# A decoder layer with 32 experts on one core: expert products in blocks of 32 slots on four column strips, and two parts of the routing stage moved into the branch stage

## The reference, cut to what matters

```python
merged = sigmoid(gate_a) * y_a + sigmoid(gate_b) * y_b
x = x + g1 * (merged @ w_out)
h2 = rms_norm(x, norm2_w) * (1 + sc2) + sh2
logits = h2 @ w_router + b_router              # 32 experts
top_val, top_idx = top_k(logits, 4); top_w = softmax(top_val)
# for each expert e, on the tokens that chose it
gate = min(h2 @ w_gate[e] + b_gate[e], 7.0)
up = clip(h2 @ w_up[e] + b_up[e], -7.0, 7.0)
y_e = ((up + 1) * gate * sigmoid(1.702 * gate)) @ w_down[e] + b_down[e]
x = x + g2 * sum_e(top_w * y_e); y = rms_norm(x, final_norm_w)
```

## Time and profile before

| what | value |
|---|---|
| median of 3 runs | 2026.03 us (2024.24 to 2029.33) |
| the profiled execution | 2019.1 us, its span 2017.4 us |
| mean granted TensorE clock | 0.929 of full speed |
| PE busy | 1803.5 us (89%) |
| DVE, ACT, POOL busy | 637.8, 301.3, 126.1 us |
| read from HBM | 486.86 MB, 245 GB/s over the span |

### The profile page before, as it was taken

One profiled execution on the slowest core, in us unless ns is written; L12 is line 12 of the kernel. 1 busy time (PEld: TensorE's weight loads), 2 busy tenths in 40 slices (PEclk: granted clock), 3 DMA queues, 4 the chain that ended last, 5 costly groups with the idle time before them and its releaser, 6 DMA issues. The chain is left out here.

```text
span 2017.4 us, 22708 instructions
## 1 busy us (share of the span) xinstructions
PE 1803.5 (89%) x8638; PEld 940.3 (47%) x8639; DVE 637.8 (32%) x1142; ACT 301.3 (15%) x521; POOL 126.1 (6%) x198
## 2 busy tenths in 40 slices
PE   6997998999879994589999999999999999999996
PEld 4775766868446762553333333333333333333332
DVE  1454333361410024733133333322332212232222
ACT  2234131110111001121011111111110100111002
POOL 1111202112100005200000000000000000000000
PEclk8998999997689997699998999999999999999997
DMA  9352162210255332049899999998999779898720
GB/s 325 129 167 84 42 233 101 84 53 1 61 184 206 117 147 96 0 192 421 311 379 414 421 422 422 422 422 342 417 417 390 298 292 365 311 410 336 250 83 28
DMA packets 114943, 494.07 MB, mean 245 GB/s; under 512 B 9931, under 2 KB 27532, under 8 KB 65687
## 3 DMA queue, kind: packets, MB, share of 16 engines
q1 hardware_dynamic: 112906, 490.69, 62.8%
q10 hardware_dynamic: 1984, 2.64, 0.4%
HBM read 486.86 MB, written 6.43 MB: 245 GB/s over the span
## 5 line engine op out<-in xcount | busy, mean ns | idle before, releaser
L1710 PE MATMUL ps_moe<-ring,hT_moe 128*64 128x512 f32 x1280 | 308.6, 641 | 0.0
L1710 PE MATMUL ps_moe<-ext,xg 128*64 128x512 f32 x1280 | 281.8, 595 | 3.5 <-DVE xg L1809 3.5
L1710 PE MATMUL ps_moe<-ring,xg 128*64 128x512 f32 x1280 | 281.7, 595 | 0.0
L739 PE MATMUL ps_mix<-hT,ring 128*128 128x320 f32 x896 | 263.2, 450 | 14.7 <-ACT cbuf L656 6.7
L739 PEld LDWEIGHTS ps_mix<-hT,ring 128*128 128x128 f32 x896 | 174.9, 198 | 90.7 <-issue 15.8
L1710 PEld LDWEIGHTS ps_moe<-ring,hT_moe 128*64 128x64 f32 x1280 | 95.4, 147 | 187.6 <-issue 185.0
L1710 PEld LDWEIGHTS ps_moe<-ext,xg 128*64 128x64 f32 x1280 | 91.8, 137 | 180.5 <-issue 177.5
L1710 PEld LDWEIGHTS ps_moe<-ring,xg 128*64 128x64 f32 x1280 | 89.2, 137 | 178.4 <-issue 178.3
L1836 DVE TENSOR_SCALAR gate<-ps_moe 128x1024 f32<-128x1024 f32 x32 | 39.2, 1224 | 233.7 <-PE ps_moe L1717 233.7
L1845 DVE TENSOR_SCALAR hid<-ps_moe 128x512 f32<-128x512 f32 x64 | 44.0, 687 | 209.8 <-PE ps_moe L1717 209.8
L1822 DVE TENSOR_SCALAR chosen<-ones,expert_row 96x64 bf16<-96x64 f32 x32 | 8.0, 250 | 313.8 <-PE ps_moe L1717 313.8
(11 more groups left out here) (354 smaller groups left out, 1711.1 us busy)
## 6 DMA issues: line engine op xcount, KB each, us to landing
ext<-in_w_gate SPq DMA_DIRECT2D x128, 1024.0 KB, 9.9
ring<-in_w_up SPq DMA_DIRECT2D x128, 1024.0 KB, 10.9
ring<-in_w_down SPq DMA_DIRECT2D x128, 1024.0 KB, 8.4
ring<-in_w_in SPq DMA_DIRECT2D x18, 2048.0 KB, 9.1
ring<-in_w_ada SPq DMA_DIRECT2D x12, 2048.0 KB, 9.3
ext<-in_state_gdn_rec SPq DMA_DIRECT2D x8, 512.0 KB, 8.4
out_rec_sample<-ext SPq DMA_DIRECT2D x8, 512.0 KB, 3.2
ring<-in_w_branch_b SPq DMA_DIRECT2D x2, 2048.0 KB, 15.0
```

The costliest lines, as they stand in the source:

```text
L739: last = nc.tensor.matmul(out, ring[:, place(i), k, P * j:P * j + P], rhs[:, k, :], start=k == 0, stop=k == NC - 1)
L1710: last = nc.tensor.matmul(ps[MID * a:MID * a + MID, bank + blk, :], lhs(blk, c), w[:, k, HALF * a:HALF * a + HALF], start=c == 0, stop=False)
```

## The change

It has two parts. In the expert loop the slots come in blocks of 32 (`STRIP`). For a block and a chunk, four matmuls run with 32 columns of tokens as weights, one for each quarter of 256 output columns (`QW`), on four column strips of the array. An expert with up to 32 tokens runs block 0 alone, one with up to 64 blocks 1 and 0, one with more blocks 1, 2, 3 and 0. The blocks run one after another, each over all 8 chunks, and only block 0, always the last, releases pieces. `put` and `wpick` are turned in two halves, one before `down` and one behind it; `hid` is always turned for all four blocks. `sums` takes the place of the pairs, with four row strips of 32.

In the routing stage, the 11 small loads, the split of the biases with the zeroing of yacc, and the squares with their sums, mean, Ln and Exp move into the branch stage: the loads to ACT's start, the split to POOL behind the turned x, the squares behind each `wo` unit. The scale and shift of h2T go chunk by chunk; the logits run on four column strips, one group per chunk, and are turned back by 3 small matmuls; S is built tile by tile of tokens, and PE starts on a tile when it is there. ACT first copies 2048 columns of x2T to PSUM (nothing reads them).

```diff
@@ branches
+    @block.gpsimd
+    def _(pool):
+        pool.wait_ge(rows_d, 9 * 16)
+        pool.wait_ge(x_s, 2 * NC)
...
+        bias_step(nc.gpsimd.tensor_copy(brow[0:3 * E], whole[0:3 * E]))
+        for g in (1, 2, 2):
+            rows = slice(E * g, E * g + E)
+            bias_step(nc.gpsimd.tensor_tensor(whole[rows], whole[rows], brow[rows], ALU.subtract))
+            bias_step(nc.gpsimd.tensor_copy(brow[rows], whole[rows]))
+        nc.gpsimd.memset(yacc[:], 0.0)
...
+        act.dma_start(wr[:], t["w_router"][0].rearrange("(c p) e -> p c e", p=P)).then_inc(ld, 16)
+        act.dma_start(br[:], t["b_router"].to_broadcast([P, E])).then_inc(ld, 16)
+        for m, name in enumerate(("b_gate", "b_up", "b_down")):
+            for g in range(3):
+                act.dma_start(whole[E * g:E * g + E, m, :], t[name][0]).then_inc(rows_d, 16)
...
+            if kind == "wo" and c >= 1:
+                add_square(c - 1)
+        add_square(NC - 1)
...
+        dve.wait_ge(sum_t, 2 * NC)
+        nc.vector.tensor_scalar(rstd[:], ps[:, 7, 0:T], 1.0 / D, EPS, ALU.mult, ALU.add).then_inc(mean_s, 1)
@@ experts, routing
-                link(nc.vector.tensor_tensor(h2T[:], x2T[:], rstd[:].unsqueeze(1).to_broadcast([P, NC, T]), ALU.mult))
...
+                link(nc.vector.tensor_tensor(h2T[:, :, SEQ:T], x2T[:, :, SEQ:T], rstd[:, SEQ:T].unsqueeze(1).to_broadcast([P, NC, T - SEQ]),
+                                             ALU.mult))
...
+                        nc.vector.scalar_tensor_tensor(out=h2T[:, c, 0:SEQ], in0=x2T[:, c, 0:SEQ], scalar=gw[:, c, 0:1],
+                                                       in1=rstd[:, 0:SEQ], op0=ALU.mult, op1=ALU.mult).then_inc(hm_s, 1)
...
+                        nc.vector.tensor_scalar(h2T[:, c - 1, 0:SEQ], h2T[:, c - 1, 0:SEQ], SH2[:, c - 1, 0:1], None,
+                                                ALU.add).then_inc(h_s, 1)
...
+                    last = nc.tensor.matmul(ps[strip:strip + STRIP, 6, 0:T], wr[:, c, :], h2T[:, c, :], start=c < NSTRIP,
+                                            stop=c >= NC - NSTRIP)
@@ experts, loop
+                def strips(m, bank, blk, lhs, wait):
+                    for c in range(NC):
+                        if c % 2 == 0:
+                            wait(4 * m + c // 2)
+                        w = raw_piece(ring, ext, 4 * m + c // 2)
+                        for q in range(Q):
+                            last = nc.tensor.matmul(ps[STRIP * q:STRIP * q + STRIP, bank + blk // 2,
+                                                       QW * (blk % 2):QW * (blk % 2) + QW],
+                                                    lhs(blk, c), w[:, c % 2, QW * q:QW * q + QW], start=c == 0, stop=False)
+                        if blk == 0 and c in (1, 3, 5):
+                            last.then_inc(piece_t, 1)
...
+                def product(i, m, bank, n_tok, b, lhs, ready=None):
+                    with pe.If(n_tok > CAP * b + STRIP):
+                        block_of(i, m, bank, 1, lhs, ready)
+                    with pe.If(n_tok > CAP * b + 2 * STRIP):
+                        for blk in (2, 3):
+                            block_of(i, m, bank, blk, lhs, ready)
+                    block_of(i, m, bank, 0, lhs, ready).then_inc(piece_t, 1)
...
+                            for q in range(Q):
+                                last = nc.tensor.matmul(ps[:, banks[q], 0:T], yrow[STRIP * q:STRIP * q + STRIP, blk, P * j:P * j + P],
+                                                        put[STRIP * q:STRIP * q + STRIP, blk, :], start=blk == 0, stop=blk == 1)
...
+                    turn_hidden(i)
+                    if not first_of_pass:
+                        pe.wait_ge(comb_s, 3 * i)
+                    pe.wait_ge(wpick_s, i + 1)
+                    turn_put(0)
+                    product(i, 2, 4, mine, b, lambda blk, c: hT[:, blk, c % 2, STRIP * (c // 2):STRIP * (c // 2) + STRIP],
+                            lambda blk: pe.wait_ge(hT_s, 3 * i + min(blk, 2) + 1))
+                    pe.wait_ge(put_s, 2 * i + 1)
+                    turn_put(1)
```

More of the change, by code:

```diff
@@ L1721, in pair @@
-                def pair(i, j, bank, blocks):
-                    for blk in range(blocks):
-                        for a in range(2):
-                            last = nc.tensor.matmul(ps[:, bank + a, 0:T], yrow[MID * a:MID * a + MID, blk, P * j:P * j + P],
-                                                    put[MID * a:MID * a + MID, blk, :], start=blk == 0, stop=blk == blocks - 1)
-                    last.then_inc(comb_t, 1)
-                def first_pairs(i, blocks):
+                def strips(m, bank, blk, lhs, wait):
+                    for c in range(NC):
+                        if c % 2 == 0:
[7 more added lines that the diff above has]
+                            last.then_inc(piece_t, 1)
@@ new lines, in block_of, with wait @@
+                def block_of(i, m, bank, blk, lhs, ready):
+                    def wait(p):
+                        pe.wait_ge(raw_full[p], 16 * (i + 1))
+                        if ready and p == 4 * m:
+                            ready(blk)
+                    strips(m, bank, blk, lhs, wait)
+                    if m == 0:
+                        pe.wait_ge(chosen_s, i + 1)
+                    for q in range(Q):
+                        last = nc.tensor.matmul(ps[STRIP * q:STRIP * q + STRIP, bank + blk // 2, QW * (blk % 2):QW * (blk % 2) + QW],
+                                                chosen[0:3 * E, :], brow[0:3 * E, m, QW * q:QW * q + QW], start=False, stop=True)
+                    return last
@@ L1753, in turn_put, with turn_hidden @@
-                def turn_put(i, blocks):
-                    pe.wait_ge(wpick_s, i + 1)
-                    for blk in range(blocks):
+                    pe.wait_ge(comb_s, 3 * i + 2)
+                    sums(i, 1, (0, 1, 6, 7), n_tok, b)
+                def turn_hidden(i):
+                    for blk, bank, at in ((0, 2, 0), (1, 5, 0), (2, 3, 0), (3, 3, 2)):
+                        if blk % 2 == 0:
+                            pe.wait_ge(hid_s, 2 * i + blk // 2 + 1)
+                        for k in range(2):
+                            last = nc.tensor.transpose(ps[:, bank, P * (at + k):P * (at + k) + P],
+                                                       adjacent(hid[:, blk, :], k), ident[:])
+                        if blk != 2:
+                            last.then_inc(turn_t, 1)
@@ L1791, in body @@
-                    by_width(mine, down)
+                        last_sums(i - 1, before, b, True)
+                    turn_hidden(i)
[5 more added lines that the diff above has]
+                            lambda blk: pe.wait_ge(hT_s, 3 * i + min(blk, 2) + 1))
```

337 lines of the change are left out of this document (156 added, 181 removed).

## The result

The changed kernel takes **2488.75 us** (2483.2 to 2492.8, 4 runs) where the kernel before took 2025.13: ratio 1.231 [1.223, 1.240]. The forecast was 1986. Rival 3, with a chance of 0.07 and a price of 2190, is what happened, at more than twice its price.

The account below looks back on a forecast made before the run. Routing was taken as unfed and all on the path, the expert loop as limited by PE and weight DMA closely together. -38 - 2 + 1.5 - 3 + 1.3 = -40 us, 2019.1 to 1979; median 1986, range 1950 to 2050.

Parts of the forecast that it names:

- Rival 3: Expert loop: its code no longer stays with PE, jumps miss in each iteration, some +200 us, 2190; chance 0.07.
- (j): Expert loop: jumps over skipped blocks cost time; one of 3.6 us charged, in the first expert: +4 (0 to 12).
- (h): Expert loop: sum by stretch of small and large experts, now against after: together -33 us.
- (a): Squares, mean, Ln, Exp moved into the branch stage: it ends 6.3 us later, 1.9 of it from seven matmuls.
- (b): Routing start to logits: L1543 starts at about 791.0 instead of 829.07, -38 us (bounds 26 and 40 gained).
- (c): S built tile by tile, zeroing of xs on POOL: PE starts earlier, DVE paces the spans; -2 us (-4 to +1).
- (d): Branch stage: added loads share the DMA with its first slot, +1.5 us (0 to 3); POOL's split nothing (up to +3).
- (e): Expert products: one block of 32 slots on four strips, bias included, takes 3.65 us (bounded above by 4.6).
- rival 2: Expert products: four-strip matmuls of 256 columns don't keep pace, some 155 us in all, 2141; chance 0.15.
- (f): Expert chains on PE: 18.9 us up to 32 tokens, 29.8 for 33 to 64, 52 for more.
- (g): Expert loop: late release shrinks the weight lead; 29.8 us DMA per expert, about +5 for a large expert starting behind.
- (i): Expert loop: granted clock falls, 2 us charged in each of 13 experts that PE paces: +26 (0 to 40).

Follow-up runs that it names:

- loop at 7988: New branch and routing stages with the old expert loop, plus three never-run stretches of 78 products: 1761 instructions, starting at PE instruction 7988; 2466.5 us.
- version of 1606: The changed kernel with only the down product of slots 64 to 127 as one block of 64 on two strips: 1973.8 us, ratio 0.974.
- pair64: The changed kernel with slots 64 to 127 as one block of 64 on two strips, 1198 loop instructions: 1960.3 us, repeated at 1962.5.
- first experiment: The changed kernel's new branch and routing stages with the old expert loop, 807 loop instructions: 1980.6 us, ratio 0.9805 to the kernel before.

## Why the prediction was wrong

**The step that failed is (j), and with it rival 3.** The forecast charged one jump of 3.6 us, +4 in all. PE waited 482 us ahead of the three products. Rival 3 named the mechanism, with 3.6 us a miss from the earlier trace rows where 4.86 were measured. It then failed at two steps. First, it held that 1860 instructions "just fit", since 7.3 lines are fewer than 8. What must fit are the lines that the loop touches and the line behind, and 1849 instructions that start at 9009 (35.2 lines) and end at 10858 (42.4), by the same compiled program as the sizes, touch 8. With the line behind they are nine. The runs show that eight lines, counted so, are kept and nine are not. The Trainium skill ("Advanced Engine Details and Errata", Sequencer Memory, ISA Cache) gives 128 KB in lines of 16 KB; worked out from that, 8 lines. The same list says "Only 2 cache lines!", and loops of 7 lines without a fetch disagree with that. "Runtime: NRT & Kernel Launch" of the Trainium skill (Instruction fetch mechanics) adds that the next block is fetched while one runs. Seven touched and one ahead are 8, so the runs agree with the two together. That the line ahead takes a place rests on two counts: nine fetches in a pass over 8 lines in the changed kernel, and the loop at 7988, which fails with 7 lines of run code where the version of 1606, with 7, is free. No run varied the line ahead alone.

Second, the price of failing was taken as three misses an expert. Once the lines don't fit, about as many are fetched in each pass as it touches: (316 - 38) / 31 passes = 9.0 fetches, and (262 - 39) / 31 = 7.2 in the dead-code run of 1761. Of the branches 109 / 31 = 3.5 a pass wait (five in most small experts, mostly one, the jump back, in a large one), 530 / 31 = 17 us a pass where 10.8 were charged, and the 10 us of cover didn't show. The granted clock of the loop falls from 0.97 to 0.81 besides. Experts 4 to 14 took 523 us where (h) had 308, 19.5 more each, and the large ones but the last 59 to 60 us each where 52 was predicted. (The sum was off as well: 10.8 us in the 13 experts that PE bounds and 0.8 in the other 19 are 156 us, not 200.)

A third point is one of judgement. The earlier trace rows showed 16 KB a fetch, the code gave a count 0.7 of a line from the limit of 8, and the penalty beyond it was not bounded. A resource at 91% with an unknown price behind it should have had more than 0.07 and a price reaching to the worst case: all 7.3 lines in each of 31 passes, at 3.6 us each, is 815 us.

**The rest held, part by part.** The kernel without the fetches is the pair64 version, span 1963.7 against the 1979 of the sum.

(a), (b) *Routing.* The mixer ended 4.7 us later in this execution already (573.26 against 568.56; the other executions have 566.7 to 577.7). Each `wo` unit with its square came 4.85 us apart against 4.31, 0.54 us more where 0.27 was said; over seven units that is 3.8 us instead of 1.9. The term was mis-sized: a unit is 8 such matmuls of 320 columns and takes 4.31 us, 0.54 each, so one more costs what the others do. The way from the last residual to the logits then took 17.1 us where 18.6 was forecast and hid it. The logits stood at 796.04 instead of 829.07, which is -33.0 as it stands and -37.7 without the 4.7 us; predicted -38. The first experiment gives the sum of (a) to (d) in the end, -42 by the medians where -38.5 was predicted. The spans give -38.3, but that they come so near is luck: this execution's mixer ended 4.5 us later, and its loop, from the first jump back to the last, was 3.2 us shorter.

(c) *S by tile.* From the first S to the last copy of xs 35.4 us against 37.3, -1.9; predicted -2.

(d) *Branch stage.* No extra wait was found at its start (PE idle for 13.16 us ahead of the first unit, before 13.31), and DVE's operations beside POOL's split stayed at 0.49 us. The 1.5 us charged were 0.

(e) *A block.* With its bias it takes 3.70 us from its start to the next work (902.18 to 905.88 in pair64) and 3.57 where another block follows, where 3.65 was predicted; rival 2 is out. In the changed kernel too, where no gap stands ahead:

```profile
2433.10 3.64 PE L1744 MATMUL ps_moe<-ring,hT_moe 128*32 128x256 f32 x64
2436.56 0.29 PE L1761 MATMUL ps_moe<-work,chosen 96*32 96x256 bf16 x4
2436.67 3.64 PE L1744 MATMUL ps_moe<-ring,hT_moe 128*32 128x256 f32 x64
```

By the rule of the Trainium skill that was weighed beside it (2.38 of 3) a block would be 4.4 us; the trace disagrees. (The 130 us that the prediction hung on it don't follow: at its own 155 us for 1.16 us a block, 0.75 us more are 100.)

(f) to (h) *Chains and stretches*, by the jumps back of the loop in the pair64 version: a small expert behind a large one 20.2 us (18.9 predicted), one of two blocks 30.8 (29.8), experts 4 to 14 309.3 us (308), 16 to 20 131.9 (129), 26 to 28 70.5 (69), the eight large ones 438.3 (439). The late release showed as predicted: in the stretches of small experts the DMA is the limit. Windows of expert 3, of experts 7 to 14 and of expert 21 there:

```profile
920.50:971.70 51.20, 49.67 (x567) 23.00 (x559) 10.35 (x17) 4.37 (x7) 0.00 (x0) 1.00 0.81 335
...
1042.90:1281.00 238.10, 192.78 (x2440) 96.96 (x2432) 82.75 (x136) 34.94 (x56) 0.00 (x0) 0.86 1.01 425
...
1472.10:1531.30 59.20, 55.01 (x567) 24.22 (x563) 10.35 (x17) 4.37 (x7) 0.00 (x0) 0.91 0.80 331
```

Expert 3 has its weights in time: 51.2 us at clock 1.00. Experts 7 to 14 run at a DMA share of 1.01, 425 GB/s. Expert 21 comes behind such a stretch, starts late and at a lower clock, and takes 8 us more; predicted +5.

(i) *Clock.* The 26 us were too much. Experts 4 to 31 sum to 949.7 us there (1921.3 - 971.6), where (g) and (h) without a clock term give 308 + 129 + 32 + 21 + 69 and 387 for seven large ones, 946. The clock did fall, to 0.92 in the loop, but where the DMA sets the pace a slower PE costs nothing; 4 us were left of 26. With that term right the forecast for code that fits would have been 1964, and 1960 and 1962 were measured.

(k) *End.* From the last bias matmul of the last `down` (2440.12) to DVE's L1932 (2456.64) 16.5 us, against 14.5 before: +2.0, predicted +1.3.

## What to carry to other kernels

Count the instructions that an engine's loop holds before writing a product out once more, and count them in 16 KB lines from the start of the program, with the line behind each one that is run: on PE eight lines ran free here, the ninth cost 470 to 530 us, all at once. A profile warns by one line, the packets of the instruction queue, and by idle time called "issue" ahead of a jump's target. Where two shapes of matmul cost the same time, as one block of 64 x 512 on two strips and two of 32 x 256 on four do, the wider one is the cheaper code; and code that is skipped belongs in one stretch outside the path and not spread between the parts that run. Only code that is never run was tried there; what it costs when it is run now and then is open.

## What was not expected of the hardware

- Never-run code costs 530 us when spread over the loop (1905 instructions, 313 fetches) and at most 7 us when it stands in one stretch (1893, 40 fetches).
- The same loop of 1761 instructions takes 2466.5 or 1983.7 us by its place in the program.
- A line without any run code, directly behind one that is run, seems to take a place too: the loop at 7988 has 7 lines of run code and nine fetches in most passes, the version of 1606 has 7 and none.
- A branch inside which a fetch lands holds PE's sequencer mostly 2 to 7 us (in the mean 4.86; 7.3 at the slow jumps back of the dead-code run of 1761), where the others take 0.2.
- Code that is run for the first time is not free either: the version of 1606 instructions has 7.36 us of "issue" ahead of expert 0's first product, which starts 3.2 us later than in the shorter one (847.50 against 844.29).
- One more float32 matmul of 128 x 128 on 320 columns costs 0.54 us at full clock, as each of the 8 in a unit does (4.31 us).
